# Block products for the last two levels of a triangular inverse, with the long convolution's taps moved later on POOL and DVE

## What is computed

```python
proj = a @ w_in                      # a (264, 1024); 56 column blocks of 128 are used
qkv  = silu(causal_dwconv(qkv_raw))  # 4 taps, 3072 channels
# gated delta rule, 8 heads, chunks of the prompt
a_mat = where(strict, (kb @ k.T) * decay, 0)
t_inv = triangular_solve(eye + a_mat, eye)         # inverse of a unit lower triangle
u, w  = t_inv @ (v*beta), t_inv @ (kb*exp(gc))
# per chunk: v_new = u - w@s ; o = qg@s + qk@v_new ; s = s*dl + kd.T@v_new
# conformer branch: causal depthwise convolution with 31 taps over 512 channels, layer norm, silu
x = x + (g_a*branch_a + g_b*branch_b) @ w_out
# top-4 of 32 experts: gate_up 1024x2048 and down 1024x1024 for each, all 32 are streamed from HBM
x = x + moe(rmsnorm(x)); x = x + (p @ w_ple_proj) * gate; y = rmsnorm(x)
```

## Time and profile before

| | us |
|---|---|
| median of 3 runs | 1493.44 (1490.57 to 1497.97) |
| the profiled execution's own time | 1489.93 |
| its span, first to last instruction | 1488.2 |
| PE busy in the span | 1368.9 (92%) |
| DVE, ACT, POOL busy | 463.2, 290.2, 112.5 |
| front: projection blocks end | 397 |

### The profile page before, as it was taken

One profiled execution on the slowest core, in us unless ns is written; L12 is line 12 of the kernel. 1 busy time (PEld: TensorE's weight loads), 2 busy tenths in 40 slices (PEclk: granted clock), 3 DMA queues, 4 the chain that ended last, 5 costly groups with the idle time before them and its releaser, 6 DMA issues.

```text
span 1488.2 us, 20223 instructions
## 1 busy us (share of the span) xinstructions
PE 1368.9 (92%) x7581; PEld 791.0 (53%) x7581; DVE 463.2 (31%) x978; ACT 290.2 (19%) x608; POOL 112.5 (8%) x183
## 2 busy tenths in 40 slices
PE   7999888999999999898898998988989889999887
PEld 6787766788888434344244342443433425534256
DVE  3555876755224402022022020220211202202224
ACT  4544425353303101000010000100100001101024
POOL 3000685300000000000000000000000000000000
PEclk9999999999999999999999999999999999999999
DMA  7423323342496799999999999999999999999950
GB/s 208 132 80 108 102 85 91 98 131 65 141 342 213 296 422 421 421 421 423 422 422 420 421 421 422 422 422 422 422 421 421 420 422 421 421 421 421 421 201 30
DMA packets 121524, 462.78 MB, mean 311 GB/s; under 512 B 10843, under 2 KB 69748, under 8 KB 72196
## 3 DMA queue, kind: packets, MB, share of 16 engines
q1 hardware_dynamic: 105147, 451.97, 76.0%
q10 hardware_dynamic: 16305, 9.82, 2.2%
HBM read 455.75 MB, written 6.68 MB: 311 GB/s over the span
## 4 chain that ended last, share of the span: by engine, by line
PE 67%; DMA 21%; DVE 5%; ACT 3%; issue 2%; SPq 0%; ACTq 0%; DVEq 0%
DMA ring<-in_w_gate_up 21%; PE bank L1126 15%; PE bank L1084 14%; PE bank L910 10%; PE bank L1042 6%; PE bank L1147 4%; PE bank L958 3%; PE bank L763 3%; PE bank L992 2%; PE bank L1198 2%; PE bank L1077 1%; PE bank L769 1%; PE bank L1106 1%; PE bank L1062 1%; PE bank L896 0%
## 5 line engine op out<-in xcount | busy, mean ns | idle before, releaser
L1084 PE MATMUL bank<-ring,lent 128*64 128x512 f32 (+1 forms) x2304 | 459.1, 595 | 66.5 <-DMA ring<-in_w_gate_up 66.4
L1084 PEld LDWEIGHTS bank<-ring,lent 128*64 128x64 f32 (+1 forms) x2304 | 147.9, 131 | 362.0 <-issue 343.1
L910 PE MATMUL bank<-lent,ring 128*128 128x264 f32 x896 | 227.6, 394 | 4.1 <-DVE big L1853 1.6
L1126 PE MATMUL bank<-ring,lent 128*64 128x512 f32 (+1 forms) x1152 | 226.7, 595 | 0.2 <-ACT lent L1554 0.2
L910 PEld LDWEIGHTS bank<-lent,ring 128*128 128x128 f32 x896 | 162.5, 193 | 36.8 <-issue 9.5
L2005 DVE TENSOR_SCALAR big<-bank 128x512 f32<-128x512 f32 x32 | 20.6, 686 | 431.4 <-PE bank L1084 431.4
L1126 PEld LDWEIGHTS bank<-ring,lent 128*64 128x64 f32 (+1 forms) x1152 | 69.8, 131 | 135.8 <-issue 128.7
L1548 ACT ACTIVATE big<-big 128x512 f32<-128x512 f32 x32 | 19.6, 630 | 511.9 <-DVE big L2005 511.9
L1042 PEld LDWEIGHTS bank<-st,big 88*128 88x128 f32 x768 | 86.9, 192 | 12.8 <-issue 11.4
L1042 PE MATMUL bank<-st,big 88*128 88x128 f32 x768 | 90.0, 277 | 0.6 <-ACT outputs L1545 0.5
L2023 DVE TENSOR_TENSOR xT<-xT,bank 128x264 f32<-128x264 f32 x128 | 54.9, 429 | 96.7 <-PE bank L1147 95.1
(11 more groups left out here) (382 smaller groups left out, 1136.8 us busy)
## 6 DMA issues: line engine op xcount, KB each, us to landing
ring<-in_w_gate_up SPq DMA_DIRECT2D x256, 1024.0 KB, 19.1
ring<-in_w_down SPq DMA_DIRECT2D x128, 1024.0 KB, 23.5
ring<-in_w_in SPq DMA_DIRECT2D x28, 1024.0 KB, 5.3
out<-st ACTq DMA_DIRECT2D x8, 512.0 KB, 3.5
ring<-in_w_gdn_out SPq DMA_DIRECT2D x4, 1024.0 KB, 5.8
ring<-in_w_out SPq DMA_DIRECT2D x4, 1024.0 KB, 9.9
ring<-in_w_ple_gate SPq DMA_DIRECT2D x4, 1024.0 KB, 15.7
st<-in_state_gdn ACTq DMA_DIRECT2D x6, 512.0 KB, 4.1
```

Of the source, the lines that this page charges most:

```text
L910: last = mm(b[:, 0:T], w[:, k, o:o + P], aT[:, k, :], start=k == 0, stop=k == KD - 1)
L1084: last = mm(bank[t][lo:hi, :], x_slots[:, c, lo:hi], w, start=False, stop=c == KD - 1)
L1126: last = mm(bank[4 + t][lo:hi, :], hT[:, m, lo:hi], w, start=m == 0, stop=m == KD - 1)
```

## The change

Two edits. **The inverse**: the loop over masks ends at side 16. Side 32 (`ad4`, `dm4`, and `dt4` in place of `tr4`) and side 64 (`adl`, `lt`) compute only the blocks that are not zero: eight products of 32x32 a step, or four of 64x64. The results are no longer added into Dm and DT by DVE but copied into place by ACT. `dt4` shares a third with `dm4`, so the plan is one entry shorter and every later step of a group, up to `ofin`, stands one third earlier. **The taps**: POOL does 20 of its 62 taps after group 1's `t1` and 42 after group 2's (48 and 14 before); DVE's slots are one in three thirds up to third 103, then four in three.

```diff
-LEVELS = [2, 4, 8, 16, 32]
+LEVELS = [2, 4, 8, 16]
...
-            ["ad3", "sc2"], ["dm3", "sc3"], ["tr3", "kv0"], ["ad4"], ["dm4"], ["tr4", "kv1"], ["adl", "store0"], ["lt"],
+            ["ad3", "sc2"], ["dm3", "sc3"], ["tr3", "kv0"], ["ad4"], ["dm4", "dt4", "kv1"], ["adl", "store0"], ["lt"],
...
+BLOCKS32 = [(slice(0, 32), slice(32, 64)), (slice(64, 96), slice(96, 128))]
...
-POOL_TAPS = {1: range(0, 48), 2: range(48, 62)}
+POOL_TAPS = {1: range(0, 20), 2: range(20, 62)}
...
-TAPS_FROM = 14
+TAPS_FROM, LATE_TAPS = 14, 104
...
     for x in range(3 * TAPS_FROM, 3 * CONF_END):
-        due += 2
-        taps[x] = int(due >= 3 and x not in busy)
+        due += 1 if x < LATE_TAPS else 4
+        taps[x] = min(due // 3, 2) if x not in busy else 0
         due -= 3 * taps[x]
...
+                elif step == "ad4":
+                    wait_drained(pe, name("dm3"))
+                    b = to_fill(pe, name(step))
+                    for i in range(4):
+                        for r, e in BLOCKS32:
+                            last = mm(b[e, 32 * i:32 * (i + 1)], AT[r, i, e], Dm[r, i, r], start=True, stop=True)
+                    fill_done(name(step), last)
+                elif step == "dm4":
+                    wait_drained(pe, name("ad4"))
+                    wait_drained(pe, name("tr3"))
+                    b = to_fill(pe, name(step))
+                    for i in range(4):
+                        for r, e in BLOCKS32:
+                            last = mm(b[e, 32 * i:32 * (i + 1)], DT[e, i, e], M[e, i, 0:32], start=True, stop=True)
+                    fill_done(name(step), last)
+                elif step == "dt4":
+                    b = to_fill(pe, name(step))
+                    for i in range(4):
+                        for r, e in BLOCKS32:
+                            last = mm(b[r, 32 * i:32 * (i + 1)], M[e, i, 0:32], DT[e, i, e], start=True, stop=True)
+                    fill_done(name(step), last)
+                elif step == "adl":
+                    wait_drained(pe, name("dm4"))
+                    b = to_fill(pe, name(step))
+                    for i in range(4):
+                        last = mm(b[64:P, 64 * i:64 * (i + 1)], AT[0:64, i, 64:P], Dm[0:64, i, 0:64], start=True, stop=True)
+                    fill_done(name(step), last)
+                elif step == "lt":
+                    wait_drained(pe, name("adl"))
+                    wait_drained(pe, name("dt4"))
+                    b = to_fill(pe, name(step))
+                    for i in range(4):
+                        last = mm(b[0:64, 64 * i:64 * (i + 1)], M[64:P, i, 0:64], DT[64:P, i, 64:P], start=True, stop=True)
+                    fill_done(name(step), last)
...
+                elif step in ("ad4", "dm4", "dt4"):
+                    b = to_drain(act, name(step))
+                    for r, e in BLOCKS32:
+                        rows = r if step == "dt4" else e
+                        x = b[rows, 0:P].rearrange("p (i c) -> p i c", i=4)
+                        if step == "ad4":
+                            x = A(M[rows, :, 0:32], x, ACT.Copy)
+                        else:
+                            x = A(Dm[rows, :, r] if step == "dm4" else DT[rows, :, e], x, ACT.Copy, scale=-1.0)
+                    out_of(x, name(step))
...
-                elif step == "lt":
-                    b = to_drain(dve, name(step))
-                    out_of(v.tensor_tensor(four(DT), four(DT), b[:], ALU.add), name(step))
```

More of the change, by code:

```diff
@@ L180 @@
 TIMETABLE = _timetable()
-CONF_SLOTS = [(i[1], i[2]) for i in TIMETABLE if i[0] == "conf_tap"]
+CONF_SLOTS = [(i[1], i[2]) for i in TIMETABLE if i[0] == "conf_tap" for _ in range(TAPS[3 * i[1] + i[2]])]
 assert len(CONF_SLOTS) >= CK * DVE_BLOCKS + CB - DVE_BLOCKS
@@ L803, in gdn_step @@
                     transposes4(name("T1"), lambda i: DT[:, i, :])
+                elif step == "ad4":
[32 more added lines that the diff above has]
+                    fill_done(name(step), last)
                 elif step[:2] == "ad":
-                    lv = len(LEVELS) if step == "adl" else int(step[2])
+                    lv = int(step[2])
                     wait_drained(pe, name(f"dm{lv - 1}" if lv else "T1"))
@@ L817, in gdn_step @@
                     transposes4(name(step), lambda i: Dm[:, i, :])
-                elif step == "lt":
-                    wait_drained(pe, name("adl"))
-                    wait_drained(pe, name(f"tr{len(LEVELS) - 1}"))
-                    products4(name("lt"), lambda i: M[:, i, :], lambda i: DT[:, i, :])
                 elif step in ("vn0", "vn1"):
@@ L1394, in gdn_step @@
                     out_of(nc.scalar.copy(Dm[:].rearrange("p i c -> p (i c)"), to_drain(act, name("T1"))), name("T1"))
+                elif step in ("ad4", "dm4", "dt4"):
[8 more added lines that the diff above has]
+                    out_of(x, name(step))
+                elif step == "adl":
+                    b = to_drain(act, name(step))
+                    out_of(A(M[64:P, :, 0:64], b[64:P, 0:2 * P].rearrange("p (i c) -> p i c", i=4), ACT.Copy), name(step))
+                elif step == "lt":
+                    b = to_drain(act, name(step))
+                    out_of(A(DT[0:64, :, 64:P], b[0:64, 0:2 * P].rearrange("p (i c) -> p i c", i=4), ACT.Copy, scale=-1.0),
+                           name(step))
                 elif step[:2] == "tr":
@@ L1726, in gdn_step @@
                     out_of(v.tensor_tensor(four(QKT), b[:], four(dec), ALU.mult), name("QK"))
-                elif step[:2] == "ad":
-                    lv = len(LEVELS) if step == "adl" else int(step[2])
+                elif step in ("ad0", "ad1", "ad2", "ad3"):
+                    lv = int(step[2])
                     b = to_drain(dve, name(step))
                     out_of(v.tensor_tensor(M[:], bank4(b), each4(neg_mask[:, lv, :]), ALU.mult), name(step))
-                elif step[:2] == "dm":
+                elif step in ("dm0", "dm1", "dm2", "dm3"):
                     b = to_drain(dve, name(step))
                     out_of(v.tensor_tensor(four(Dm), four(Dm), b[:], ALU.add), name(step))
-                elif step == "lt":
-                    b = to_drain(dve, name(step))
-                    out_of(v.tensor_tensor(four(DT), four(DT), b[:], ALU.add), name(step))
                 elif step == "ks":
@@ L2160, in _ @@
             tell(g_.memset(neg_mask[:], 0.0))
-            for lv, side in enumerate(LEVELS + [P // 2]):
+            for lv, side in enumerate(LEVELS):
                 n = P // (2 * side)
@@ L2168, in _ @@
                                       pattern=[[2 * side, n], [0, side]], channel_multiplier=-1),
-                     "masks_ready" if lv == len(LEVELS) else None)
+                     "masks_ready" if lv == len(LEVELS) - 1 else None)
             def gdn_step(g, step):
```

## The result

The changed kernel takes 1501.68 us in the median of four runs (1501.31 to 1505.89), the kernel before 1493.29 us on the same chip: a ratio of 1.0059 with a 95% interval of [1.0038, 1.0079]. It is slower, since the interval leaves out 1; whether the loss is more than the half per cent that the forecast took as the least that can be told, the interval does not decide. The forecast was 1494.0 us in a range of 1483 to 1504: the measured time lies inside the range, and the change that can be told was not forecast.

A forecast was written before the change was run, and what follows sets the result against it. PE in the front, held by chains through DVE and ACT, was taken as the bound. Products -1.0, group 1 -7.4, group 2 +3.0 and transitions +6.0 sum to +0.6 us: 1494.0 us forecast, range 1483 to 1504.

The forecast's parts named there:

- taps, group 1: Group 1: fewer taps remove 4.85 us of PE waits and 3.3 of low clock, one tap adds 0.75; -7.4 us.
- taps, groups 0, 2 and 3: Later taps: +3.0 us for DVE's in group 2, 1.75 for the slower sample part between groups 2 and 3.
- products: Last two inverse levels: small products and visits take 3.9 against 4.17 us a group; -1 us for four.
- table loads and what follows: Between groups: six ACT table loads replace three as onorm moves ahead; 0.6, 1.85 and 1.85 us later.
- The first term: Group 2, thirds 105 to 108: four more DVE taps ahead of dm1's addition, 0.745 us each; +3.0 us.
- from third 109 on the extra taps meet idle time: Group 2: DVE's idle time there (26.32 of 34 us busy) covers further taps while it lasts; cost nothing.
- the sample part: Between groups 2 and 3: its seven ACT instructions slow beside POOL, 3.9 us at most; 1.75 taken.
- POOL and DVE choke group 2: Rival, chance 0.13: from 280 us on, PE idles up to 6 us and loses 3 to clock; 1503.5 us.
- One sign that I had named: Group 2: PE's waits at tr0 and tr1 would be near 3.4 and 3.9 us.
- the price of a visit: Small-product steps: 1.7 us for 48 records, 0.9 for 16 half-size, 1.3 for edges of four visits; sum 3.9.
- the rival had 100: Rival, small products do not overlap, chance 0.10: 0.10 us a record in the inverse's last levels; 1506.5 us.
- The transitions: Between groups: added ACT table loads delay the next group by 0.6, 1.85 and 1.85 us, sample part aside.

The follow-up runs named there:

- t_only: The kernel before with only the taps moved as in the changed kernel; 1500.74 us, ratio 1.0037.
- aligned: The changed kernel with one empty third ahead of the output normalisation's squares, restoring their old place; 1493.73 us, ratio 0.9980 to the kernel before.
- dve_late: aligned_p with DVE's taps alone moved as in the changed kernel; 1487.40 us, ratio 0.9934 to the kernel before.
- aligned_p: The changed kernel with the old taps and an empty third ahead of the output normalisation's squares; 1486.62 us, ratio 0.9947 to the kernel before.
- warm: The changed kernel with unused matmuls ahead of the broadcasts of groups 1, 2 and 3; 1500.36 us, ratio 1.0037 to the kernel before.
- p_only: The changed kernel with all taps as in the kernel before; 1497.07 us, ratio 1.0004 to the kernel before.
- dve_undone: The changed kernel with DVE's taps alone put back as in the kernel before; 1493.26 us, ratio 0.9986 to the kernel before.
- pool_late: aligned_p with POOL's taps alone moved as in the changed kernel (20 and 42); 1481.70 us, ratio 0.9899 to the kernel before.
- pool_27: aligned_p with POOL's taps 27 in group 1 and 35 in group 2; 1479.51 us, ratio 0.9901 to the kernel before.

## Why the prediction was right or wrong, point by point

Three kernels in a row, each one edit from the last, take the sum apart: before, *t_only* (the taps), *aligned* (the products), after (the place of the output normalisation).

| part | forecast | measured |
|---|---|---|
| taps, group 1 | -7.4 | -7.7 |
| taps, groups 0, 2 and 3 | +3.0 + 1.75 | +14.5 |
| products | -1.0 | -7.3 |
| table loads and what follows | +0.6 + 1.85 + 1.85 | +8.65 |
| sum | +0.6 | +8.2 |

The ratios of the same kernels give +5.5 for the taps, -8.5 for the products and +11.8 for the last part, so each line is known to some 3 us.

**Group 1's taps: right**, in size and in mechanism. The waits at the last transpositions and at `ks` are gone, and from 176 to 222 us TensorE waits for nothing. In *t_only* the stretch has 4.2 us less idle and 3.5 us less busy time than before; the forecast had 4.85 of waits less 0.75 for a tap, and 3.3 for the clock.

**Group 2's taps: the step that failed.** The first term was right: from the broadcast to `ob` *dve_late* takes 47.69 us and *aligned_p* 44.72, +3.0 us. Wrong was the sentence that from third 109 on the extra taps meet idle time of VectorE and cost nothing. That idle time (26.32 of 34 us busy) was read where GpSimd's taps were running out, while thirds 109 to 126 got 25 slots for VectorE's taps where they had 15; beside GpSimd's 42 the cover is gone. With 1.75 us for the sample part the forecast had 4.75 us there, and *t_only* shows 13.0 in group 2, 7.2 of them as TensorE's lower clock, for which I had put nothing in group 2. The rival "POOL and DVE choke group 2" named this place and put it at +9 to 10, of which 3 for the clock; I gave it 0.13. Shown is that it needs both engines' taps (1.7 and 3.0 us alone, 11.5 together). I had counted as evidence against it that VectorE has lost four passes a group; with them gone the later taps still cost 11.5 us in group 2. One sign that I had named failed too: TensorE's second wait there, said to be near 3.9 us, was 2.10.

**The products: right in sign, wrong in size, and outside my bounds.** The term that was mis-sized is the price of a visit, records and edges both. The small records took 17 to 23 ns where I took 35 and set 27.5 as the least: 0.90 us for 48, not 1.7. The half-size ones took 1.20 us and not 0.9. Edges cost 0.19 us at three places, 0.57 and not 1.3: `dm4` and `dt4` stand with `kv1`, which changes the shape anyway, and 0.14 us on entering is not to be seen. And the first full product behind the old chain took 0.67 us (in the chain of waits before, at 128.89 us), now 0.44. (0.90 + 1.20 + 0.57) - (4.17 + 0.23) = -1.73 us a group, -6.9 for four, against 7.1 and 7.3 measured. In group 0, where TensorE hardly waits, its busy time falls by 1.85 us from *t_only* to *aligned*. The row that I took as the least, 32 or 8 weight columns at 27.5 ns, has all 128 rows of the array in use, and the new records have 32; that this is the reason is not shown.

The Trainium skill, "TensorEngine Tiling (Array Packing)", "Gotcha 1: PSUM Pressure", says that different row tiles cannot access the same PSUM bank simultaneously. Here two row tiles write one bank, at 17 to 23 ns a record where the rival had 100; whether the two ever write at the same moment the trace does not tell. The same page of the Trainium skill, "Key Properties", says that changing the tiling mode drains TensorE. The trace agrees at the edge behind (1.53 us where 1.34 is usual), and shows nothing of it ahead.

**The transitions: right in mechanism, half in size.** The forecast was 4.3 us, measured are 8.65. Nine loads more, as forecast, and a wait of 4.49 us at the broadcast of group 2 where I had "some 4". I counted how much later ScalarE ends and not what TensorE does after idling that long. The clock falls behind each of the three waits, the projection rows there are 6.55 us longer together (1.78 + 2.58 + 2.19), and between groups 1 and 2 it is TensorE that ends last, since ScalarE waits 3.17 us for it at 243.42. From *aligned* to the changed kernel TensorE's busy time in the four stretches grows by 6.2 us (297.82 to 304.00) and its idle time by 2.5. That is where the 8.65 us appear, not what each is worth: *warm* had only some 3 us less. How the rest divides was not separated. With other taps the same place costs 14.8 us (*p_only* against *aligned_p*; 8.5 by the ratios) or 8.0 (*dve_undone* against *pool_late*; 13 by the ratios), so the size is known to a few us only.

**The total** came within 8 us by luck: two errors of opposite sign, -6.3 at the products and +9.7 at the taps of groups 0, 2 and 3 (8.2 of it in group 2), took most of each other away. What was left, with +4.3 at the transitions, is the miss. The chance of 0.21 for slower was put on dear products and a choked group; the second of them occurred.

## What to carry to other kernels

An engine's idle share covers moved work only under the load that its neighbours have in the same place: look at both engines' busy time where both get work. A wait that the move makes can cost as much again in TensorE's clock. When a step is dropped from a plan, look at what the steps behind it now stand beside. The one empty third that restores the old order is worth at least as much here as the products (8.65 and 7.3 us in the table, 11.8 and 8.5 by the ratios). And ask of a stretch of slow neighbours not only how long it is but which steps with a waiter it covers.

## What the hardware showed that I had not expected

VectorE's steps grow beside GpSimd by very different factors: a tap of 128x256 from 0.48 to 0.72 to 0.91 us, a 128x48 step from 0.21 to 0.66 or 0.77 us, more than three times, while a step that reads a PSUM bank (L1784, 128x256) takes 0.42 us either way (beside GpSimd's taps at 305.92 us in the changed kernel, without them at 209.78 us in *pool_27*). GpSimd's own instructions there take 0.61 to 0.68 and 0.72 to 0.79 us, about what the small steps come to. The Trainium skill, "SBUF — State Buffer", section "Who interferes with whom", has this as a rule: a VectorE instruction with two SBUF inputs contends with a GpSimd instruction that reads SBUF, one with at most one SBUF input does not. The trace agrees in both halves. TensorE's clock fell after an idle time of 2.33 us (the projection behind it 5.51 us for 3.73), and in *warm* after one of 0.84 us too, with work of no use in front of it. In the kernel before it did not fall after one of 2.61 us: the four transposes behind it took 0.66 us, and the granted clock from 246 to 280 us was 1.00. So the length of the last wait alone does not say whether it falls. Records of 32x32 on two tiles ran at 17 to 23 ns each.
